# A two-stack transformer kernel: the modulation slabs of the first stack's attention taken by twos, in every second or third unit

## What is computed

```python
# first stack, each layer l of 2
u = rmsnorm(h, attn_norm[l])
(aq, ak, av, iq, ik, iw, bq, bk, bv, cq, ck, cv, gates) = split_columns(u @ w_in)
o_a = dsa_attention(...)          # 6 heads; the 128 best keys of each query by an indexer's score
o_b = dilated_attention(...)      # 12 heads in three groups, joined by their log-sum-exp
o_c = sink_window_attention(...)  # 8 heads, window of 128, with sinks
g = jax.nn.sigmoid(gates.reshape(Bsz, L, N_BRANCHES, D_MODEL))
merged = g[:, :, 0] * (o_a @ w_a) + g[:, :, 1] * (o_b @ w_b) + g[:, :, 2] * (o_c @ w_c)
h = h + merged @ w_o
h = h + jnp.square(jax.nn.relu(rmsnorm(h, mlp_norm[l]) @ w_up[l])) @ w_down[l]

# second stack, each layer l of 2: modulation of latents and context
mod_lat = (silu_c @ w_ada[l] + b_ada[l])      # 1024 x 6144 weights, one row of input
mod_ctx = silu_cc @ w_ada[l] + b_ada[l]
```

## Time and profile before

| | |
|---|---|
| median of 3 runs | 3530.51 us (3529.26 to 3533.37) |
| profiled execution | 3533.22 us, of which the span 3531.1 us |
| granted TensorE clock, mean of the profiled execution | 0.989 |
| TensorE busy | 3426.7 us, 97% of the span |
| VectorE, ScalarE, GpSimd busy | 2094.1, 1347.6, 188.5 us |
| moved by DMA | 317.26 MB, 90 GB/s in the mean |

### The profile page before, as it was taken

One profiled execution on the slowest core, in us unless ns is written; L12 is line 12 of the kernel. 1 busy time (PEld: TensorE's weight loads), 2 busy tenths in 40 slices (PEclk: granted clock), 3 DMA queues, 4 the chain that ended last, 5 costly groups with the idle time before them and its releaser, 6 DMA issues.

```text
span 3531.1 us, 53461 instructions
## 1 busy us (share of the span) xinstructions
PE 3426.7 (97%) x20094; PEld 2796.5 (79%) x20094; DVE 2094.1 (59%) x3321; ACT 1347.6 (38%) x2115; POOL 188.5 (5%) x45
## 2 busy tenths in 40 slices
PE   8999999999999999999999999999999989999998
PEld 6766888888777678888878777888888877788887
DVE  7876557444678745645566654653544665566546
ACT  6546333222454553322223554341323235534322
POOL 2321000000133010000000000000000001000000
PEclk9999999999999999999999999999999999999999
DMA  3245233222222633332221001121121110112222
GB/s 142 84 156 204 103 112 107 95 95 95 84 95 85 239 121 119 116 109 95 96 95 49 13 13 56 49 72 60 60 72 58 62 72 14 56 65 103 96 95 84
DMA packets 45782, 317.26 MB, mean 90 GB/s; under 512 B 5008, under 2 KB 7312, under 8 KB 8464
## 3 DMA queue, kind: packets, MB, share of 16 engines
q1 hardware_dynamic: 44576, 307.01, 24.3%
q10 hardware_dynamic: 1008, 7.50, 0.5%
HBM read 312.39 MB, written 2.10 MB: 89 GB/s over the span
## 4 chain that ended last, share of the span: by engine, by line
PE 83%; DVE 9%; ACT 3%; DVEq 2%; issue 2%; DMA 1%; POOL 0%; SPq 0%; ACTq 0%; POOLq 0%
PE psum L731 21%; PE psum L732 21%; PE psum L735 21%; PE psum L1380 4%; PE psum L1412 2%; PE psum L1397 2%; DVE MA L2353 2%; PE psum L815 1%; PE psum L1215 1%; PE psum L878 1%; PE psum L1348 1%; DVE BQK L2117 1%; DVEq L2112 1%; ACT whi L1596 1%; PE psum L1207 1%
## 5 line engine op out<-in xcount | busy, mean ns | idle before, releaser
L731 PE MATMUL psum<-xh,whi 128*128 128x512 f32 (+1 forms) x2224 | 857.2, 388 | 3.0 <-issue 2.0
L732 PE MATMUL psum<-xl,whi 128*128 128x512 f32 (+1 forms) x2224 | 851.0, 385 | 0.0
L1596 ACT ACTIVATE whi<-wst 128x2048 fp32r<-128x2048 f32 x233 | 445.1, 1910 | 578.2 <-PE psum L735 553.9
L2099 DVE TENSOR_TENSOR wlo<-wst,whi 128x2048 fp32r<-128x2048 f32 x199 | 456.0, 2291 | 175.2 <-ACT whi L1596 173.7
L735 PE MATMUL psum<-xh,wlo 128*128 128x512 f32 (+1 forms) x2224 | 536.4, 383 | 0.1
L731 PEld LDWEIGHTS psum<-xh,whi 128*128 128x128 f32 x2224 | 420.1, 189 | 95.5 <-issue 13.8
L732 PEld LDWEIGHTS psum<-xl,whi 128*128 128x128 f32 x2224 | 420.2, 189 | 82.2 <-issue 1.0
L735 PEld LDWEIGHTS psum<-xh,wlo 128*128 128x128 f32 x2224 | 409.8, 188 | 82.3 <-POOL wlo L693 0.5
L693 POOL TENSOR_TENSOR wlo<-wst,whi 128x2048 fp32r<-128x2048 f32 x40 | 187.8, 4695 | 2871.4 <-ACT whi L1956 1769.0
L731 PE MATMUL psum<-uh,whi 128*128 128x512 f32 x480 | 189.8, 395 | 0.0
L732 PE MATMUL psum<-ul,whi 128*128 128x512 f32 x480 | 189.5, 395 | 0.0
(11 more groups left out here) (373 smaller groups left out, 5726.1 us busy)
## 6 DMA issues: line engine op xcount, KB each, us to landing
wst<-weights SPq DMA_DIRECT2D x287, 1024.0 KB, 4.8
dft<-c_dft ACTq DMA_DIRECT2D x2, 2688.0 KB, 10.5
hT<-x_t SPq DMA_DIRECT2D x4, 512.0 KB, 8.1
wst<-weights SPq DMA_DIRECT2D x2, 512.0 KB, 5.9
cT<-ctx_t ACTq DMA_DIRECT2D x1, 1024.0 KB, 7.0
out<-hT SPq DMA_DIRECT2D x1, 1024.0 KB, 4.9
out<-hT SPq DMA_DIRECT2D x2, 512.0 KB, 3.0
masks<-c_masks SPq DMA_DIRECT2D x1, 644.0 KB, 11.4
```

The source lines that it names most:

```text
L731: pe.matmul(out, weights(m.whi, k), head(k), start=opens and n == 0, stop=False)
L732: pe.matmul(out, weights(m.whi, k), tail(k), start=False, stop=False)
L1596: act.activation(m.whi[:, slot, :], m.wst[:, slot, :], ACT.Copy).then_inc(s.hi_ready, 1)
L2099: TT(m.wlo[:, slot, :], m.wst[:, slot, :], m.whi[:, slot, :].bitcast(F32), ALU.subtract).then_inc(s.lo_ready, 1)
```

## The change

`ADA_AT` now gives two slabs to each of twelve units: 0, 3, 6, 9, 12, 15, then 17, 19, 21, 23, then 25 and 28. The two products stand one behind the other on TensorE, and ScalarE waits for both and raises the semaphores after each. The new function `gathered(u)` says which gathering is filled in unit u; the first is full in unit 15 instead of 16, the second in unit 28 instead of 30, so the columns come in iterations 16 and 29 instead of 17 and 31. The number of slabs, of instructions on `wst`, and of loads is the same, and both layers of the first stack use the same table.

```diff
@@ -107,10 +107,15 @@
 
 
 ADA_AT = {}
-for _u in [0] + [u for u in range(FIRST_B) if u % 3] + list(range(FIRST_B, FIRST_A)) + [
-        FIRST_A + n for n in (0, 1, 3, 4, 6)]:
-    ADA_AT[_u] = len(ADA_AT)
-assert len(ADA_AT) == ADA_SLABS
+for _u in list(range(0, FIRST_B, 3)) + list(range(FIRST_B + 1, FIRST_A, 2)) + [FIRST_A + 1, FIRST_A + 4]:
+    ADA_AT[_u] = (2 * len(ADA_AT), 2 * len(ADA_AT) + 1)
+assert 2 * len(ADA_AT) == ADA_SLABS
+
+
+def gathered(u):
+
+
+    return ADA_AT[u][1] // GATHER if u in ADA_AT and (ADA_AT[u][1] + 1) % GATHER == 0 else None
 
 
 GATHER = 12
@@ -125,8 +130,8 @@
             for c in range(chunks_of(u)):
                 at["T", u, c] = n
                 n += 1
-        if (ADA_AT.get(u - 1, 0) + 1) % GATHER == 0:
-            at["cols", ADA_AT[u - 1] // GATHER] = n
+        if gathered(u - 1) is not None:
+            at["cols", gathered(u - 1)] = n
             n += 1
     return at, n
 
@@ -916,7 +921,8 @@
                     if u == 0:
                         done_steps = 2
                         pe.wait_ge(s.acc_free, l * FREES1 + FR_C + 4 + 5)
-                        rows_of(l, ADA_AT[0])
+                        for k in ADA_AT[0]:
+                            rows_of(l, k)
                     while done_steps < min(STEPS1, last_step + 3):
                         logits(l, done_steps)
                         done_steps += 1
@@ -935,10 +941,10 @@
                         turn(l, u, c)
                     if u:
                         denominators(l, u - 1)
-                    if (ADA_AT.get(u - 1, 0) + 1) % GATHER == 0:
-                        columns_of(l, ADA_AT[u - 1] // GATHER)
-                    if u and u in ADA_AT:
-                        rows_of(l, ADA_AT[u])
+                    if gathered(u - 1) is not None:
+                        columns_of(l, gathered(u - 1))
+                    for k in ADA_AT.get(u, ()) if u else ():
+                        rows_of(l, k)
 
             def relevance(l, k):
 
@@ -1647,17 +1653,15 @@
 
             def modulation(l, u):
 
-                k = ADA_AT.get(u - 1, 0)
-                if (k + 1) % GATHER == 0:
-                    a = k // GATHER
+                a = gathered(u - 1)
+                if a is not None:
                     at = RING["cols", a]
                     act.wait_ge(s.t_done, l * RING1 + at + 1)
                     mods = m.mods[:, l, 4 * GATHER * a:4 * GATHER * (a + 1)].rearrange("p (k t s) -> p t k s", t=2, s=2)
                     cols = ps[4 + at % 2][:, 0:4 * GATHER].rearrange("p (t k s) -> p t k s", t=2, s=2)
                     act.activation(mods[:, 0, :, :], cols[:, 0, :, :], ACT.Copy)
                     act.activation(mods[:, 1, :, :], cols[:, 1, :, :], ACT.Copy).then_inc(s.t_copied, 1)
-                if u in ADA_AT:
-                    k = ADA_AT[u]
+                for k in ADA_AT.get(u, ()):
                     act.wait_ge(s.ada_done, l * ADA_SLABS + k + 1)
                     act.sem_inc(s.hi_ready, 1)
                     act.sem_inc(s.lo_ready, 1)
```

## The result

The changed kernel takes 3541.19 us in the median of 20 runs (3533.49 to 3547.13), the kernel before on the same chip 3534.47 (3528.92 to 3539.34, 20 runs). The ratio is 1.0019, with an interval of 1.0013 to 1.0026: 6.7 us slower, between 4.6 and 9.2. The forecast was 1.5 us slower. The forecast started from 3530.51, the median of three runs; these are three of the 20, and their median lies 4 us under that of all.

The account below looks back on a forecast made before the run. VectorE and ScalarE pace the units up to 12, TensorE units 13 to 24; 0.9 + 0.2 + 1.4 + 0.2 - 1.2 = +1.5 us on the median 3530.51 gives 3532.0 us, range 3527 to 3539.

Parts of the forecast that it names:

- Slab 21's load: Unit 25, second load of a pair: taken to land 5.9 us after issue, at 316.1 us, so that TensorE waits.
- one after the other: Rival: two loads move successively, each as fast as alone; second lands 6.9 us after issue; 3534 us, chance 0.10.
- bound of 6.7 us: Upper bound on a slab load's time, read from one of two loads that overlap by half; a lone load takes 4.8.
- Its price: ScalarE's copy of unit 26's transposes comes later by +0.9 us in the first layer, +1.4 us in the second.
- hand-over: Around unit 12, where TensorE becomes the limit: ten slabs done at 266.0 instead of 266.52 us, counted as -0.35 us.
- The clock at the start: Start of the second layer's attention: shorter TensorE idling, 2.70 us, keeps the clock from falling; -1.2 us, other end 0.
- C pairs at 0: Pairs in units 3, 6, 9, 12, 15: the longer block is hidden by 0.3 us of slack, so no time is lost.
- vector chain held up: Rival, iteration behind a pair in C units: ScalarE's copy waits, up to 1.00 us a pair; 3540 us, chance 0.13.
- Denominators of unit 23: Unit 23, first layer: the denominators that release VectorE's chain, 311.12 us before, come 0.65 us later.
- Slabs 22 and 23: Unit 28: ScalarE waits for the second slab before its copies and unit 30's exponential; +0.2 us a layer.
- TensorE's waits vanish: Rival, TensorE's idle time from 223 to 266 us is lost time; removing it gains 9.0 us; 3521.5 us, chance 0.07.

Follow-up runs that it names:

- half loads: The change with loads of slabs 18 to 23 moving only each slab's first half, against the kernel before: ratio 1.0002 (0.9993 to 1.0011), +0.7 us.

## Why the prediction was wrong, step by step

- **Slab 21's load, "I take the other of these two, 5.9": the step that failed.** It measured 7.3 and 7.0 us in the first trace of the change, 6.2 and 6.4 in the second. The value was chosen by the start's mean of 349 GB/s, "6.0 us for two slabs". That was a slip of its own: 6.0 us for two counts from the first issue, which is 5.0 from the second's. And a mean over 13.7 us spreads a load's fixed part over many loads, while two of them pay it in full: 4.8 for the first and 2.5 more for the second, 7.3 from the first issue, so 6.1 to 6.3 from the second's when it comes 1.0 to 1.2 us later. The rival *one after the other* has this mechanism, which the half loads show; its 6.9 from the second's issue was too much by the typical pair, though nearer to the first trace. It had 0.10; it should have been the forecast.
- **What this leaves over.** In the first layer of the first trace 1.2 us of the 7.3 remain, and they are no matter of two loads sharing the way. Each load of a slab ends with sixteen packets of under 512 B in the trace of the DMA. Of slab 21's, fifteen had come by 318.6 us, and the last came at 319.87. From 318.33 to 318.60 and from 318.60 to 318.94 us the view shows:

```profile
DMA packets 14, 0.01 MB, mean 31 GB/s; under 512 B 13, under 2 KB 13, under 8 KB 13
...
DMA packets 1, 0.01 MB, mean 24 GB/s; under 512 B 0, under 2 KB 0, under 8 KB 0
```

  One part of sixteen was 1.3 us behind the rest. In the change's second trace all sixteen of this load lie within 0.5 us, and the load took 6.2. Why one lags stays open, and so do the 1.0 us that remain of the second layer's 7.0. The forecast's bound of 6.7 us, "one of two that overlap by half", was misread too: it is the first of the two, issued at 248.3 us, 5.5 us behind the load before it, and its last closing packet came 1.3 us behind the fifteenth.
- **Its price.** In the first layer of the first trace the copy of unit 26 was 3.3 us late instead of 0.9. The 2.4 us between: 0.4 because the load was issued later, in part since unit 23's second slab came late too (its load took 6.6 us, and there were 6.5); 1.4 from the load itself; 0.6 because the clock fell behind the wait and stretched logits and transposes ahead of the copy (321.22 to 322.88, 1.66 us instead of 1.1). In the second layer the copy was 1.3 late, with the clock 0.7 us better up to unit 12: 2.0 against the forecast's 1.4. One late slab thus cost in three ways, of which the forecast had one. In the second trace the same copies were 1.5 and 1.4 us later than in the mean of the kernel before's two traces.
- **By the experiments.** The forecast's terms for the last three pairs come to +3.4 (its 0.9, 0.2, 1.4 and 0.2, and the 0.35 of the hand-over in each layer, which is in them), and the change's attentions are 7.4 and 5.3 us longer than those of the version without these pairs. Its terms for the other nine come to -1.9, and that is what this version has in its one trace, though the clock's gain is not among its parts: that sum came out by luck.
- **The clock at the start, -1.2: wrong too.** In the second layer a part of it came in the first trace: the denominators of unit 12 are 43.1 us into the attention instead of 43.8, behind 2.84 us of idleness instead of 3.70. In the second traces it was the other way (44.2 for the change, 43.5 for before). In the first layer the forecast had the clock hold, and there all six traces with pairs in units 0 and 3 have 0.86 in the mean from 224 to 248 us, though TensorE idles only 2.0 us ahead of unit 1's transposes. What follows is thinner, since units 1 and 2 have no slab; that this is why was not shown. Of the seven traces with slabs one by one, behind 2.87 us of idleness, four have 0.93 and three 1.00. The idle time alone, by which the forecast judged, did not decide.
- **C pairs at 0.** Right: 9.03 us for three units, and the version with these pairs alone loses nothing. A pair took 1.87 us rather than 2.0. The *vector chain held up* did not happen in the C units; it happened in unit 25, and in unit 23 of the version with the last pairs only, for a load.
- **Hand-over, -0.35.** Right in sign as far as one trace tells: with pairs in C units only, the attention is 0.6 us a layer shorter, the falls of the clock included.
- **Denominators of unit 23, +0.65.** With half loads they are 0.5 us later than before in the first layer (88.2 us into the attention against 87.7); in the change 1.0.
- **Slabs 22 and 23, +0.2.** From the copy to the end the second layer lost 0.2, the first 0.6 with the slower clock. With half loads the attentions are within 0.3 us of the kernel before's mean.
- ***TensorE's waits vanish*:** without the last three pairs the attentions are 1.9 us shorter in sum, where this rival wanted 9.
- **The absolute time.** Range and forecast stood on 3530.51 us; over 20 runs the kernel before took 3534.47. The range ended 8.5 us over its base, the result lies 6.7 over its own, so as a difference it is inside; as a time, 3541.19, it is above 3539. Of the 5.2 us between forecast and result as differences, 4.0 lie in the attentions by the first trace and 1.9 by the second; the rest is outside them, where the forecast had nothing, and stays open.

## What to carry to other kernels

Where two buffers feed a consumer, putting the uses side by side puts the loads side by side as well: the first comes as before, the second one whole movement later. Count the budget from slot free to next use for the *second* of a pair, and take the slow end of the loads seen (6.2 to 7.9 us here), not the middle. Then look who stands behind the late product in program order: here ScalarE waited for a product it did not need for its exponential, and so a late modulation slab stopped the attention. One unit's more distance, an edit of two numbers, removed the wait.

## What was not expected of the hardware

- Two 1 MB loads issued 0.87 us apart on one queue: the first lands in 4.8 us in the median, the second in 6.6 (6.3 to 7.9), 2.5 us after the first in the median, which is some 420 GB/s. The forecast cited a limit of 358 GB/s for loads from HBM from the Trainium skill (DMA: Bandwidth & Descriptors, Where 436 GB/s comes from). The measurement decides against it for one core alone: 7.3 us from the first issue instead of the 7.9 that the forecast worked out from it. Another page of the Trainium skill (Perfetto Trace Analysis, Roofline) says that a single active core can pull more than that share, up to some 435 GB/s; the 420 agree.
- A load with none issued in the 3.9 us before it takes 4.8 us in the median, but 16 of 344 in the attentions of all traces took 6.1 to 7.1 us, both kernels' among them (6.7 us in the kernel before, 7.1 in the change). In fourteen of the sixteen the last of the sixteen closing packets came 0.9 to 2.4 us behind the one before it, as with slab 21; in ordinary loads it is 0.04 us in the median. And in all sixteen a packet or two of instructions (8 or 16 KB) moved between issue and landing, as in this one, issued at 1236.04 us in the change and landed 7.14 us later (the packets, MB and share of each kind in that time):

```profile
q1 hardware_dynamic: 290, 2.11, 81.8%
q8 instruction: 1, 0.02, 0.8%
```

  Of the 187 such loads without one, none took over 5.7 us; of the 157 with one, 141 were ordinary too. So it goes with slow loads and does not make each slow, and slab 21's load of 7.3 us had none. The cause stays open.
- The kernel before's order kept the clock at 2.4 GHz through its first units in one execution (1.00) and lost it for a while in another (0.93). The Trainium skill (TensorE: Matmul & The Clock Gate, What's actually happening) calls the number of matmuls at the low clock at a kernel's start run-variable for one and the same kernel; these rows show the like for a fall in mid-kernel. In the C units a fall costs little: unit 12 was reached at 42.5 instead of 41.8 us in the kernel before's two traces.
